# Expert stage with nine weight slots instead of six, unrolled pairs, and down weights issued by ScalarE

## The reference, cut to what matters

```python
def expert_block(args):                       # 64 or more assignments are padded to blocks
    xblk, e = args
    hid = jax.nn.silu(xblk @ w_gate[e]) * (xblk @ w_up[e])   # 1024 -> 512, twice
    return hid @ w_down[e]                                   # 512 -> 1024
...
y = jax.ops.segment_sum(yb * buf_w[:, None], buf_tok, num_segments=N + 1)[:N]
```

## Time and profile before

| what | value |
|---|---|
| median of 3 runs | 1373.03 us (1369.36 to 1373.8) |
| profiled execution, its own time | 1365.32 us |
| its span, first to last instruction | 1363.5 us |
| TensorE busy | 1125.4 us, 83% |
| VectorE, ScalarE, GpSimd busy | 408.0, 218.3, 164.8 us |
| transfers | 311.73 MB, mean 229 GB/s |
| of which SyncE's queue | 273.79 MB |
| first expert product | starts 839.63 us |
| last expert product | 1325.31 to 1332.40 us |
| mean granted TensorE clock | 0.927 |

### The profile page before, as it was taken

One profiled execution on the slowest core, in us unless ns is written; L12 is line 12 of the kernel. 1 busy time (PEld: TensorE's weight loads), 2 busy tenths in 40 slices (PEclk: granted clock), 3 DMA queues, 4 the chain that ended last, 5 costly groups with the idle time before them and its releaser, 6 DMA issues. The chain is left out here.

```text
span 1363.5 us, 16892 instructions
## 1 busy us (share of the span) xinstructions
PE 1125.4 (83%) x7001; PEld 566.0 (42%) x7001; DVE 408.0 (30%) x694; ACT 218.3 (16%) x443; POOL 164.8 (12%) x235
## 2 busy tenths in 40 slices
PE   2699999999997897989799964987778878777880
PEld 0343344544465555979544541332222322222330
DVE  4524436622005444345432444100000010111004
ACT  2101123220003552324200210000000000000002
POOL 1100001124001444223100001000000000000002
PEclk9999999879998997989999976988998998999895
DMA  9512326334324004200174242999999999999985
GB/s 339 212 65 93 123 93 246 125 138 131 105 80 132 1 2 180 78 2 4 70 275 172 106 155 67 429 427 429 429 430 432 431 430 431 430 431 430 430 361 201
DMA packets 61337, 311.73 MB, mean 229 GB/s; under 512 B 6195, under 2 KB 12677, under 8 KB 48729
## 3 DMA queue, kind: packets, MB, share of 16 engines
q1 hardware_dynamic: 49784, 273.79, 50.0%
q0 software_dynamic: 9184, 32.82, 6.3%
q10 hardware_dynamic: 2304, 4.20, 0.8%
HBM read 285.11 MB, written 24.64 MB: 227 GB/s over the span
## 5 line engine op out<-in xcount | busy, mean ns | idle before, releaser
L2299 PE MATMUL ps<-ring,zrT 128*64 128x512 f32 x1024 | 254.5, 655 | 72.4 <-DMA ring<-in_moe_w_gate_dram 32.0
L2299 PEld LDWEIGHTS ps<-ring,zrT 128*64 128x64 f32 x1024 | 83.3, 150 | 232.0 <-issue 200.2
L867 PE MATMUL ps<-ring,uT 128*128 128x512 f32 x384 | 169.8, 599 | 1.2 <-PE ps L867 0.6
L2321 PE MATMUL ps<-ring,mg 128*64 128x512 f32 x512 | 116.8, 610 | 23.4 <-DMA ring<-in_moe_w_down_dram 20.7
L858 PE MATMUL ps<-uT,ring 128*128 128x512 f32 x256 | 113.9, 602 | 1.3 <-ACT uT L293 0.7
L867 PEld LDWEIGHTS ps<-ring,uT 128*128 128x128 f32 x384 | 72.4, 192 | 93.0 <-issue 93.0
L2114 DVE TENSOR_TENSOR zrT<-zrT,ps 128x512 f32<-128x512 f32 x16 | 11.0, 688 | 326.6 <-PE ps L2299 326.6
L1928 ACT ACTIVATE zrT<-ps 128x512 f32<-128x512 f32 x16 | 9.6, 597 | 435.9 <-PE ps L2299 435.9
L2321 PEld LDWEIGHTS ps<-ring,mg 128*64 128x64 f32 x512 | 38.5, 140 | 91.3 <-issue 91.2
L858 PEld LDWEIGHTS ps<-uT,ring 128*128 128x128 f32 x256 | 48.4, 192 | 66.3 <-issue 65.2
L1856 POOL DMA_DIRECT2D y_dram<-zrT x16 | 9.1, 569 | 459.2 <-DVE zrT L2124 459.2
(11 more groups left out here) (355 smaller groups left out, 1278.2 us busy)
## 6 DMA issues: line engine op xcount, KB each, us to landing
ring<-in_moe_w_gate_dram SPq DMA_DIRECT2D x32, 2048.0 KB, 19.1
ring<-in_moe_w_up_dram SPq DMA_DIRECT2D x32, 2048.0 KB, 18.3
ring<-in_moe_w_down_dram SPq DMA_DIRECT2D x32, 2048.0 KB, 19.8
ring<-in_w_ada_dram SPq DMA_DIRECT2D x12, 2048.0 KB, 9.5
ring<-in_w_in_dram SPq DMA_DIRECT2D x9, 2048.0 KB, 13.3
y_dram<-zrT POOLq DMA_DIRECT2D x16, 512.0 KB, 10.5
y_dram<-zeros POOLq DMA_DIRECT2D x1, 7680.0 KB
gates_dram<-gst ACTq DMA_DIRECT2D x16, 256.0 KB, 2.0
```

The source lines that it names most:

```text
L867: ins = pe.matmul(ps[:, n % 4, :], uT[:, k, P * i:P * i + P], w, start=(k == 0), stop=(k == KD - 1))
L2299: ins = pe.matmul(ps[HALF * r:HALF * r + HALF, "gu".index(kind), :], xgT[:, b % 2, k, HALF * r:HALF * r + HALF], w[r][:, k, :], start=(k = ...
L2321: ins = pe.matmul(ps[HALF * r:HALF * r + HALF, 2 + c, :], hdT[:, j, HALF * r:HALF * r + HALF], w[r][:, j, 512 * c:512 * c + 512], start=(j ...
```

## The change

The ring has nine slots. The three new ones are tiles that stand unused in the expert stage: rows 1 to 4 of `mod` (slot 6), `mg` (slot 7) and `uT` (slot 8); `hdT` gets a tile of its own. Their first use waits for what was done in these tiles before. The loops over pairs are written out on all engines, and registers, `turn`, `pairs` and the semaphore `e_seen` go. The down weights of pair 0 are still issued by SyncE; those of pairs 1 to 15 are issued by ScalarE behind its evacuation for the pair before.

```diff
-R = 6
+R = 9
+R2 = 6
...
-            return ring[:, s_, :] if s_ < RP else more[0][:, s_ - RP, :]
+            return ring[:, s_, :] if s_ < RP else more[0][:, s_ - RP, :] if s_ < R2 else more[s_ - R2 + 1]
...
+        more += [mod[:, 1:5, :].rearrange("p a n -> p (a n)"), mg[:, :, :].rearrange("p i n -> p (i n)"),
+                 uT[:, :, :].rearrange("p k t -> p (k t)")]
+        hdT_ = alloc(top, "hdT", [P, EH])
...
-        order = (1, 2, 0, 5, 3, 4)
+        order = (1, 2, 0, 5, 3, 4, 6, 7, 8)
...
-                s_, before = place_of(kind, b, half, it)
-                wait(eng, unit_free[s_], before + fills[s_])
-                e_ = 2 * b + half if it is None else 4 * it + (2 * b + half)
+                s_, turns = place_of(kind, b, half)
+                if turns == 0 and s_ == 6:
+                    eng.wait_ge(n2_u, NT)
+                elif turns == 0 and s_ == 7:
+                    eng.wait_ge(n2_row, 16 * NT)
+                    eng.wait_ge(n2_uT, 2 * NT)
+                elif turns == 0 and s_ == 8:
+                    eng.wait_ge(r_tab, 1)
+                    eng.wait_ge(r_ov, 1)
+                else:
+                    eng.wait_ge(unit_free[s_], turns + fills[s_])
+                e_ = 2 * b + half
...
-                with sp.Fori(0, LOOPS) as it:
-                    for b in (2, 3):
-                        for kind in "gud":
-                            load_expert(sp, kind, b - (kind == "d"), it)
-                load_expert(sp, "d", NPAIR - 1)
+                for b in range(2, NPAIR):
+                    for kind in "gu":
+                        load_expert(sp, kind, b)
...
                 silu(0)
-
-                def pair(it, half):
-                    silu(1, it)
-                    finish(0, it)
-                    silu(2, it)
-                    finish(1, it)
-
-                pairs(act, pair)
-                silu(NPAIR - 1)
-                finish(NPAIR - 2)
+                for b in range(1, NPAIR):
+                    silu(b)
+                    finish(b - 1)
+                    load_expert(act, "d", b)
                 finish(NPAIR - 1)
...
-                pairs(pe, pair)
-                product("g", NPAIR - 1)
-                hidden(NPAIR - 2)
-                product("u", NPAIR - 1)
-                down(NPAIR - 2)
+                for b in range(1, NPAIR):
+                    product("g", b)
+                    hidden(b - 1)
+                    product("u", b)
+                    if b + 1 < NPAIR:
+                        tokens(b + 1)
+                    down(b - 1)
                 hidden(NPAIR - 1)
                 down(NPAIR - 1)
```

More of the change, by code:

```diff
@@ L154, in build @@
         fills[where[n]] += 1
-    fills[R - 1] += 1
+    fills[R2 - 1] += 1
     fills[0] += 1
@@ L301, in store @@
                     eng.wait_ge(s_row, 16 * (i + 1))
-            return square, mean, root, gain, rows, turned, evacuate, store, s_ev
+            return square, mean, root, gain, rows, turned, evacuate, store, s_ev, s_u, s_uT, s_row
         mixers = top.enter_context(ExitStack())
@@ L1758, in wait @@
         def wait(eng, s_, v):
-            if not isinstance(v, int) or v > 0:
+            if v > 0:
                 eng.wait_ge(s_, v)
[L1762 to L1770, removed]
         def further(eng, first, body):
@@ L1841, in _, with gather @@
                 pool.wait_ge(m_g, 16)
[L1843 to L1848, removed]
+                def gather(b):
+                    q_ = b % 2
+                    wait(pool, e_xT, b - 1)
+                    pool.tensor_copy(idx[:, q_:q_ + 1], slots[:, b:b + 1]).then_inc(e_idx, 1)
+                    pool.wait_ge(e_idx, b + 1)
                     pool.indirect_dma_start(xg[:, q_, :], None, u2_dram,
@@ L1851, in gather, with store @@
                         .then_inc(x_in[q_], 16)
[L1853 to L1856, removed]
+                def store(b):
+                    pool.wait_ge(e_y, 2 * b + 2)
+                    pool.dma_start(y_rows[b], yo[:, b % 2, :]).then_inc(y_st[b % 2], 16)
                 pool.wait_ge(r_sl, 1)
@@ L1860, in _ @@
                 gather(1)
-                def pair(it, half):
[L1863 to L1868, removed]
+                for b in range(NPAIR):
+                    if b + 2 < NPAIR:
+                        gather(b + 2)
                     store(b)
@@ L2129, in _ @@
                 tokens(1)
[L2131 to L2142, removed]
+                for b in range(1, NPAIR):
+                    gated(b)
+                    if b + 1 < NPAIR:
+                        tokens(b + 1)
+                    finish(b - 1)
+                finish(NPAIR - 1)
                 def first():
@@ L2276, in _, with tokens @@
                 ins.then_inc(r_tab, 1)
[L2278 to L2281, removed]
+                def tokens(b):
+                    pe.wait_ge(x_in[b % 2], 16 * (b // 2) + 16)
+                    wait(pe, e_xe, b)
                     src = xg[:, b % 2, :].rearrange("t (p k) -> t k p", k=KD)
@@ L2285, in tokens, with product @@
                     ins.then_inc(e_xT, 1)
[L2287 to L2291 removed]
+                def product(kind, b):
+                    w = need_expert(pe, kind, b)
                     if kind == "g":
[L2293 to L2294 removed]
+                        pe.wait_ge(e_xe, b + 1)
+                        wait(pe, e_sl, b)
                     else:
[L2296 removed]
+                        wait(pe, e_hd, b)
                     for k in range(KD):
@@ L2302, in product, with hidden @@
                     ins.then_inc(e_g if kind == "g" else e_u, 1)
[L2304 to L2307, removed]
+                def hidden(b):
+                    pe.wait_ge(e_hd, b + 1)
+                    wait(pe, e_he, b)
                     src = hd.rearrange("t (p j) -> t j p", j=4)
@@ L2311, in hidden, with down @@
                     ins.then_inc(e_hT, 1)
-                def down(b, it=None):
-                    n = turn(it, b)
-                    w = need_expert(pe, "d", b, it)
-                    pe.wait_ge(e_he, n + 1)
-                    wait(pe, e_y, 2 * n)
+                def down(b):
+                    w = need_expert(pe, "d", b)
+                    pe.wait_ge(e_he, b + 1)
+                    wait(pe, e_y, 2 * b)
                     for c in range(2):
@@ L2323, in down @@
                         ins.then_inc(e_d, 1)
-                tokens(0, 0)
+                tokens(0)
                 product("g", 0)
                 product("u", 0)
-                tokens(1, 0)
-                def pair(it, half):
-                    for b in (1, 2):
-                        product("g", b, it)
-                        hidden(b - 1, it)
-                        product("u", b, it)
-                        tokens(b + 1, half + 1, it)
-                        down(b - 1, it)
-                pairs(pe, pair)
-                product("g", NPAIR - 1)
-                hidden(NPAIR - 2)
-                product("u", NPAIR - 1)
-                down(NPAIR - 2)
+                tokens(1)
+                for b in range(1, NPAIR):
+                    product("g", b)
+                    hidden(b - 1)
+                    product("u", b)
+                    if b + 1 < NPAIR:
+                        tokens(b + 1)
+                    down(b - 1)
                 hidden(NPAIR - 1)
```

65 lines of the change are left out of this document (29 added, 36 removed).

## The result

The changed kernel takes 1400.89 us, median of 4 runs (1398.26 to 1403.5), against 1371.19 us of the kernel before (four runs; the three listed before the prediction had 1373.03): **ratio 1.022, 95% interval 1.020 to 1.025**. Slower by 30 us where 4 us faster was forecast; the range ended at 1378. The profiled execution took 1398.26 us, its span 1396.6 us.

The account below looks back on a forecast made before the run. The expert stage was taken as bound by the transfer of weights. Three early slots gain 14.6 us, the stage's end reduces this to 4.4 us net: 1373.0 - 4.4 = 1368.6 us, range 1358.4 to 1378.

Parts of the forecast that it names:

- Part 1, nine slots: Expert stage: three weight loads issued early, at about 802, 811 and 833 us, make the last weights land 14.6 us earlier.
- Part 2, the queue and the end of the stage: Stage end: down weights on ScalarE's queue delay up 15, with three products behind it; net gain 4.4 us remains.
- the forecast's sum: Whole kernel: net 4.4 us faster, 2 to 8 by the bounds; gain of 2 to 9 us given 0.50.
- the half of the rate: Stage end: the engines serve both weight queues alternately, so down weights get 50% of the transfer rate.
- the third that was kept for the rival: Weight queues: down weights get only 32% of the rate, as service favours SyncE's queue a little.
- the whole-gain rival: Stage end: down 15 doesn't get ahead of up 15; 14.6 us faster, 1358.4 us; chance 0.18.
- Part 3, the gathers: GpSimd's gathers: landing could go from 15.0 to 25.4 us, costing up to 2.4 of TensorE's 8 us to spare.
- my own bound of 25.4 us: GpSimd's gathers competing with two weight queues: 4.6 + 2 x 10.4 us from issue to landing.
- The slower rival: Expert stage: down weights starve on ScalarE's queue; up to 5 us slower, 1377 us; slower by over 4.1 us: 0.16.
- No net gain by a lower rate: Expert stage: rate falls by 1%, 4.6 us, where both queues run; 1373 us; no net gain: 0.16.
- Written-out pairs: Loops over pairs: fetching the longer code beside saturated transfer engines costs nothing.

Follow-up runs that it names:

- e1_sp9: Changed kernel with the down weights of pairs 1 to 15 issued by SyncE again, nine slots kept; 1355.22 us, ratio 0.987 to the kernel before.
- e3_act9_early: Changed kernel with GpSimd issuing each gather one pair earlier, ahead of the store; queues and slots unchanged; 1363.41 us, ratio 0.994 to the kernel before.
- e7_act9_swap: Changed kernel with GpSimd's gather issued ahead of the store, behind the same down product; 1361.50 us, ratio 0.993 to the kernel before.
- e8_tail_sp: e3_act9_early with the down weights of pairs 14 and 15 back on SyncE's queue; 1357.21 us, ratio 0.990 to the kernel before.
- e5_sp6: e1_sp9 with six slots instead of nine, so written-out pairs alone; 1373.57 us, ratio 1.001 to the kernel before.

## Why the prediction was wrong

- **Part 1, nine slots.** Right, within 2 us at the front (issues at 801.64, 812.86, 833.16 for about 802, 811, 833) and in size: 14.6 us forecast, 13.8 in the stage of e1_sp9, 16.2 by its medians.
- **Part 2, the queue and the end of the stage.** Right in mechanism, hidden in the changed kernel by the loop. There, up 15 (1341.77), down 14 and down 15 run back to back, released by nothing that is transferred:

```profile
1341.77 7.09 PE L2272 MATMUL ps<-ring,zrT 128*64 128x512 f32 x32
...
1348.69 7.04 PE L2292 MATMUL ps<-ring,hdT 128*64 128x512 f32 x32
...
1356.44 0.60 ACT L1925 ACTIVATE hdT<-ps 128x512 f32<-128x512 f32 x1 [13.97 <-PE ps L2282]
...
1357.29 7.09 PE L2292 MATMUL ps<-ring,hdT 128*64 128x512 f32 x32 [0.89 <-ACT hdT L1925]
```

  Where the loop was cut, in e3_act9_early, the stage is 4.4 us shorter than before, the very number of the forecast's sum; the medians say 8.0, the far end of its bounds.

  That it is the very number is partly luck, for terms of the sum were off and cancelled. The gate weights of pair 15 were in at 1288.2 (1258.33 and 29.9 us to landing), as forecast with the 1.5 us added (1287.8). But TensorE came late to them: up 14 had waited 6.23 us and run 9.29, to 1283.6, and down 13 ran behind it, so the gate product ended at 1298.5 instead of 1294.9 to 1296.6. Down 15 was issued at 1299.34, some 3 us later than in the sum, and overlapped less of up 15. Nor did the down weights get the half of the rate that the sum gave them. The two loads of down 14 landed 13.8 and 15.9 us after their issue, and the median of those into the ring is 14.6; at half of 430 GB/s the bytes of one need 9.8 us, at a third 14.6. By this estimate most loads had less than a half, nearer the third that was kept for the rival, and still the whole-gain rival, which hung on that third, didn't happen.
- **Part 3, the gathers. This is the step that failed.** It put the slower landing right: 15.0 to as much as 25.4 us, and 21.7 was measured. It then said that "the tokens are wanted some 23 us after the issue (three products and the transposes), so up to 2.4 us of TensorE's 8 to spare". Both halves are wrong. Between one down product and the next transposes of tokens lie two products and one transpose, 14.9 us, not three products, and the first 2.5 us of them are past when the gather is issued (1089.07 and 1091.54), so the tokens are wanted 12.3 us after the issue when no weight is waited for, and 17.80 in the period of the kernel before shown above: the down product of the pair comes behind the transposes, as the order of TensorE's work in the code says. And the wait isn't paid out of a pair's spare time, since the next gather isn't issued before this down product has been stored: the delay goes round in a loop, whose length has to be compared with the 31.7 us of a pair. By the trace of the kernel before it is 26.4 us; with the 12.1 us of the changed kernel behind the landing it is 27.1, and turns into the bound at a landing of 19.6 us. With my own bound of 25.4 us this would have given 37.5 us a pair and, over the 13 pairs whose gather stands behind a store, 75 us on top of the forecast; with 21.7 (33.8 us a pair, 34.7 in the mean of the trace) 27 to 39 us. Between e3_act9_early and the changed kernel there are 36.4 us of stage and 37.5 of median.
- **Rivals.** None of them was this one. The slower rival had the down weights starve; they landed in 15.5 to 18.3 us (medians of the page). It would have been seen from the same inputs: I asked which transfer loses to the new queue, and answered it for the weights that were moved, and only in passing for GpSimd's, which has smaller rows than the weights (4 KB beside 16 KB) and whose next issue hangs on its own consumer one pair later.
- **No net gain by a lower rate.** With a second queue and nobody waiting for tokens, e3_act9_early moved 427 GB/s from 850 to 1300 us against 429 before, e7_act9_swap 425, and e8_tail_sp reaches the time of one queue. That bound wasn't needed. The sign that I had named for this rival, a mean rate below 425 GB/s, did show in the changed kernel (400), but from another cause: the loads were held up by TensorE, which waited for tokens. A low rate alone doesn't tell which.
- **Written-out pairs.** Nothing that can be told, as said (e5_sp6).

## What to carry to other kernels

When transfers are moved to another queue, list the transfers that stay and look which of them closes a loop: from its issue, over who consumes it, back to the next issue. Add up that loop with the new latency and compare it with the period of the stage; slack of the waiting engine doesn't pay for it. And in one queue, issue the transfer that somebody waits for ahead of the one that nobody does: here the order of two issues was worth 39 us.

## What the runs showed that I had not expected

- Two 0.5 MB transfers of one queue beside two saturated ones: first 12 us, second 21 us, whichever is the gather. Beside one weight queue the second takes 15.5, beside two 21.7. I had read 15.0 us as the price of a gather; 9 to 10 of the 21.7 are its place in the queue.
- The Trainium skill (DMA: Bandwidth & Descriptors, Issuing engines are not separate DMA queues) says that issuing from several engines saves no more than the sequencer's issue time. For the total rate the trace agrees, 427 GB/s with two weight queues (e3_act9_early) and 429 with one. What the sentence doesn't cover is the transfers that stay on the other queues: the same bytes, issued by SyncE alone or by SyncE and ScalarE, are 46 us apart (e1_sp9 and the changed kernel). The Trainium skill (same page, Queues, rings and completion order) also says that a transfer engine takes its queues in turn, packet by packet. The traces agree in direction: down weights take 14.6 us from issue to landing on a queue of their own, gate and up weights on the full queue 30 to 38 us (e3_act9_early). They don't show an even split.
